# A two-layer transformer block on one core: the second layer's first attention turns its weights three steps behind the scores

## The reference, cut to what matters

```python
def diff_attend(q, k, v, lam):
    s = jnp.einsum('bqhmd,bkhmd->bhmqk', q, k).astype(jnp.float32) * (A_QK ** -0.5)
    p = jax.nn.softmax(s, axis=-1)
    a = p[:, :, 0] - lam * p[:, :, 1]
    return jnp.einsum('bhqk,bkhd->bqhd', a, v.astype(jnp.float32))
...
o = lax.map(lambda qb: diff_attend(qb, k_all, v_all, lam), q_blocks)
out_a = diff_attention_post(o, subln, lam_init).astype(px.dtype) * jax.nn.silu(ga)
out_b = short_conv(bb, cb, ub, conv_w) * jax.nn.silu(gb)
...
oc = diff_attend(qc.reshape(B, L, A_HEADS, 2, A_QK), kc, vc, lam)
```

## Time and profile before

| | |
|---|---|
| Time, median of 3 runs | 1456.33 us (1453.93 to 1456.85) |
| Profiled execution, its time | 1454.62 us |
| Profiled execution, its span | 1452.8 us |
| TensorE busy | 1321.8 us, 91% |
| VectorE, ScalarE, GpSimd busy | 660.0, 625.3, 445.8 us |
| Mean granted clock of TensorE | 0.965 |
| The attention's 48 steps | 767.2 to about 973 us |

### The profile page before, as it was taken

How to read it: one execution, slowest core, us unless ns; L and a number is a source line. 1 busy time by engine, 2 the same in 40 slices (tenths; PEclk the granted TensorE clock), 3 DMA queues, 4 the chain that set the end, 5 groups by cost and what they waited for, 6 DMA issues and landing times.

```text
span 1452.8 us, 19794 instructions
## 1 busy us (share of the span) xinstructions
PE 1321.8 (91%) x7300; PEld 1026.2 (71%) x7300; DVE 660.0 (45%) x1276; ACT 625.3 (43%) x1323; POOL 445.8 (31%) x360
## 2 busy tenths in 40 slices
PE   7999798999999987859998999999998699999995
PEld 6767576676668665648877777778886578677774
DVE  2244784665521505252085676561621721565423
ACT  4434222665442225342226566653433522655432
POOL 2324233322234331322222333332232233222331
PEclk9999899999999998969999999999999799999998
DMA  4212143110143261434123422002121342121441
GB/s 182 84 58 88 59 169 129 64 45 30 59 145 116 105 257 62 171 110 137 59 80 105 109 65 79 30 33 85 59 102 58 131 145 87 59 88 59 175 116 58
DMA packets 27870, 139.89 MB, mean 96 GB/s; under 512 B 4096, under 2 KB 5760, under 8 KB 15232
## 3 DMA queue, kind: packets, MB, share of 16 engines
q1 hardware_dynamic: 20640, 115.43, 22.9%
q10 hardware_dynamic: 7136, 23.19, 4.9%
HBM read 122.87 MB, written 6.29 MB: 89 GB/s over the span
## 4 chain that ended last, share of the span: by engine, by line
PE 70%; DVE 11%; ACT 8%; issue 4%; DMA 3%; POOL 2%; SPq 1%; ACTq 0%; DVEq 0%; POOLq 0%
PE psum L607 48%; PE psum L635 4%; DMA w_raw<-stream 2%; POOL w_low L1079 2%; PE psum L746 2%; ACT q_masked L1250 2%; PE psum L595 2%; ACT w_high L1229 2%; PE psum L830 2%; PE psum L926 1%; PE psum L816 1%; PE psum L1023 1%; PE psum L1037 1%; PE psum L677 1%; PE psum L910 1%
## 5 line engine op out<-in xcount | busy, mean ns | idle before, releaser
L1079 POOL TENSOR_TENSOR w_low<-w_raw,w_high 128x512 fp32r<-128x512 f32 x296 | 390.3, 1329 | 851.4 <-ACT w_high L1229 851.1
L1229 ACT CAST w_high<-w_raw 128x512 fp32r<-128x512 f32 x296 | 178.4, 621 | 485.9 <-PE psum L607 336.1
L607 PE MATMUL psum<-x_high,w_high 128*128 128x512 f32 (+1 forms) x600 | 254.7, 424 | 17.1 <-DVE k_low L1868 8.9
L607 PE MATMUL psum<-x_low,w_high 128*128 128x512 f32 (+1 forms) x600 | 239.4, 399 | 0.0
L607 PE MATMUL psum<-x_high,w_low 128*128 128x512 f32 (+1 forms) x600 | 239.4, 399 | 0.0
L607 PEld LDWEIGHTS psum<-x_high,w_high 128*128 128x128 f32 (+1 forms) x600 | 113.3, 189 | 68.9 <-issue 30.5
L607 PE MATMUL psum<-w_high,x_high 128*128 128x512 f32 (+1 forms) x352 | 141.4, 402 | 13.3 <-ACT w_high L1229 7.6
L607 PE MATMUL psum<-w_low,x_high 128*128 128x512 f32 (+1 forms) x352 | 137.7, 391 | 0.0
L607 PE MATMUL psum<-w_high,x_low 128*128 128x512 f32 (+1 forms) x352 | 137.5, 391 | 0.0
L607 PEld LDWEIGHTS psum<-x_high,w_low 128*128 128x128 f32 (+1 forms) x600 | 113.2, 189 | 28.2
L607 PEld LDWEIGHTS psum<-x_low,w_high 128*128 128x128 f32 (+1 forms) x600 | 113.4, 189 | 21.0 <-issue 1.4
(11 more groups left out here) (312 smaller groups left out, 2459.0 us busy)
## 6 DMA issues: line engine op xcount, KB each, us to landing
w_raw<-stream SPq DMA_DIRECT2D x98, 1024.0 KB, 4.8
x_kept<-arena ACTq DMA_DIRECT2D x8, 512.0 KB, 4.2
arena<-x_kept ACTq DMA_DIRECT2D x8, 512.0 KB, 5.7
arena<-bias ACTq DMA_DIRECT2D x8, 512.0 KB, 3.9
q_masked<-e_q_high SPq DMA_DIRECT2D x24, 96.0 KB, 2.2
arena<-x SPq DMA_DIRECT2D x4, 512.0 KB, 5.2
arena<-x ACTq DMA_DIRECT2D x4, 512.0 KB, 6.9
arena<-ctx ACTq DMA_DIRECT2D x4, 512.0 KB, 4.8
```

Source lines behind the costliest of these rows:

```text
L607: mm = pe.matmul(o, l, r, start=(first and n == 0 and kind != "fc"), stop=(last and n == len(passes) - 1))
L1079: pool.tensor_tensor(WL[:, u % ROOM, :], RAW[:, g % 2, u % 4, :], WH[:, u % ROOM, :].bitcast(F32), ALU.subtract).then_inc(w_lo, 1)
L1229: act.copy(WH[:, u % ROOM, :], RAW[:, g % 2, u % 4, :]).then_inc(w_hi, 1)
```

## The change

The turn of a step, with its copy on ScalarE, goes from two steps behind its score to three. The values of a duo go from even steps to the odd ones that follow. A fourth buffer of the first map, in `TAB`, takes turns with the three of `E_P`; the exponential of the first map then waits for the turn of step s-4. Behind the steps there is one more turn to place among the units of `gc`; the last values stand behind unit 5 instead of unit 3, and the pairs of `ms` behind units 5, 6 and 7 instead of 4, 5 and 6.

```diff
@@ -480,7 +480,8 @@
         six_of = lambda q: [q[:, j, 0:S] for j in range(4)] + [q[:, 2 * n:2 * n + 2, S:] for n in range(2)]
         six_wide = lambda t: [t[:, i, :] for i in range(4)] + [pair(t[:, i, :]) for i in range(4, 6)]
         SIX = (0, 1, 4, 2, 3, 5)
-        map_place = lambda s, m: E_P[:, 3 + s % 2 if m else s % 3, 0:keys_of(s)]
+        FIRST_MAPS = [E_P[:, n, :] for n in range(3)] + [TAB.rearrange("p a n -> p (a n)")]
+        map_place = lambda s, m: (E_P[:, 3 + s % 2, :] if m else FIRST_MAPS[s % 4])[:, 0:keys_of(s)]
 
 
 
@@ -930,31 +931,35 @@
             pieces, n = (piece for chunk in SLIM for piece in slim(chunk)), len(EVEN)
             for s in range(n):
                 score_even(s)
-                if s >= 2:
-                    turn_even(s - 2, 0)
-                if s >= 4 and s % 2 == 0:
-                    values_even((s - 4) // 2)
+                if s >= 3:
+                    turn_even(s - 3, 0)
+                if s >= 5 and s % 2:
+                    values_even((s - 5) // 2)
                 feed("e", pieces, FEED_E[s % 4][0])
-                if s >= 2 and EVEN[s - 2][0]:
-                    turn_even(s - 2, 4)
+                if s >= 3 and EVEN[s - 3][0]:
+                    turn_even(s - 3, 4)
                 feed("e", pieces, FEED_E[s % 4][1])
 
 
             pool[0] = APART_E
+            turn_even(n - 3, 0)
+            unit("gc", 0, X, C)
+            turn_even(n - 3, 4)
+            unit("gc", 1, X, C)
             turn_even(n - 2, 0)
             values_even(n // 2 - 2)
-            unit("gc", 0, X, C)
+            unit("gc", 2, X, C)
             turn_even(n - 2, 4)
-            unit("gc", 1, X, C)
+            unit("gc", 3, X, C)
             turn_even(n - 1, 0)
-            unit("gc", 2, X, C)
+            unit("gc", 4, X, C)
             turn_even(n - 1, 4)
-            unit("gc", 3, X, C)
-            values_even(n // 2 - 1)
-            for k in range(4, NK):
+            for k in range(5, NK):
                 unit("gc", k, X, C)
-                if k < NK - 1:
-                    for i in range(2 * (k - 4), 2 * (k - 4) + 2):
+                if k == 5:
+                    values_even(n // 2 - 1)
+                if k >= 5:
+                    for i in range(2 * (k - 5), 2 * (k - 5) + 2):
                         pe.wait_ge(sig("sq"), i + 1)
                         key = ("ms", SIX[i])
                         acc = open_bank(key, 4 + i % 2)
@@ -1564,8 +1569,8 @@
 
             def exps_even(s, m):
                 key, w, c = ("e", "S", s, m), keys_of(s), 2 * (s % 4) + m
-                if m == 0 and s >= 3:
-                    filled(act, ("e", "T", s - 3, parts_of(s - 3)[-1]))
+                if m == 0 and s >= 4:
+                    filled(act, ("e", "T", s - 4, parts_of(s - 4)[-1]))
                 if m == 1 and s >= 2:
                     act.wait_ge(sig("e_p"), s - 1)
                 act.wait_ge(sig("e_neg"), 2 * s + m + 1)
@@ -1598,27 +1603,30 @@
 
             n = len(EVEN)
             for s in range(n):
-                if s >= 2:
-                    turned_even(s - 2, 0)
+                if s >= 3:
+                    turned_even(s - 3, 0)
                 exps_even(s, 0)
                 exps_even(s, 1)
-                if s >= 2 and EVEN[s - 2][0]:
-                    turned_even(s - 2, 4)
-                if s >= 4 and s % 2 == 0:
-                    values_even((s - 4) // 2)
+                if s >= 3 and EVEN[s - 3][0]:
+                    turned_even(s - 3, 4)
+                if s >= 5 and s % 2:
+                    values_even((s - 5) // 2)
                 if s:
                     fed_even(s - 1)
                     high(fed["e"][2 * s - 1] + ROOM)
             gate_units = UNITS["gc"]
+            turned_even(n - 3, 0)
+            high(fed["e"][2 * n - 1] + ROOM)
+            turned_even(n - 3, 4)
+            high(gate_units[0] + ROOM)
             turned_even(n - 2, 0)
             values_even(n // 2 - 2)
-            high(fed["e"][2 * n - 1] + ROOM)
+            high(gate_units[1] + ROOM)
             turned_even(n - 2, 4)
-            high(gate_units[0] + ROOM)
+            high(gate_units[2] + ROOM)
             turned_even(n - 1, 0)
-            high(gate_units[1] + ROOM)
+            high(gate_units[3] + ROOM)
             turned_even(n - 1, 4)
-            high(gate_units[2] + ROOM)
             values_even(n // 2 - 1)
             act.wait_ge(sig("conv_in_read"), 8)
             act.dma_start(E_BROW, dram["rows"][4:5, :].broadcast_to((P, D))).then_inc(sig("gate_rows0_in"), 16)
```

## The result

The changed kernel takes 1446.62 us (median of 5 runs, 1444.81 to 1448.83) against 1456.33 (5 runs, 1451.64 to 1456.87): ratio 0.9942, interval 0.9923 to 0.9961. A second comparison gave 1446.05 against 1453.69 (23 runs of before): 0.995, interval 0.9931 to 0.9969. So the change takes 7 to 10 us off, 0.5 to 0.6%. One execution of an experiment, the profiled one of the fourth buffer alone, was disturbed as a whole (6,002 us), so its trace is not read.

What follows compares the result with a forecast made beforehand. TensorE, busy for 91% of the span, was taken as the bound, so only its work or waiting counts. 7.0 us gained in attention less 3.2 before `e_ga` gave 3.8: 1456.33 to 1452.5, range 1448.5 to 1457.7.

Steps and rivals of the forecast that it cites:

- The start: Attention before the first pair's step 4: one turn less there, 0.24 us off.
- first stretches: Score of pair step 4 to that of step 10, four times: 25.3 instead of 26.57 us, 5.08 off in all.
- The chain by way of GpSimd's low weights: Pair step 4: low weights (2.54 us) delay the second map's scaling, then VectorE's difference; the turn waits 1.17.
- second stretch: Score of pair step 10 to the next pair's step 4: 0.58 us off 25.15, three times, 1.74 together.
- The 0.6 for turns of six transposes in place of turns of two: Cost counted against the gain between step 10 and the next pair's step 4: 0.6 us at most per moved turn.
- the tail: End of `gc`: ScalarE's sigmoids come late behind the last means, so `e_ga` waits 3.2 us, bounds 1.8 and 4.8.
- the 0.51: Behind the attention's last score: the late wait for a turn's bank, 0.51 us, goes.
- The clock: Rival, chance 0.12: the wait before `e_ga` makes the clock fall to half, 1454.1 us; 1450.9 if only the old fall vanishes.
- No tail wait: Rival, chance 0.17: sigmoids come in time before `e_ga`, all 7.0 us are kept, 1449.3.
- Waits handed on: Rival, chance 0.15: scores after step 6 wait for VectorE's queue instead, step 4 to 10 gains nothing, 1457.7 us.
- slower: Rival, chance 0.09: the attention gains nothing, the 3.2 us wait before `e_ga` stands alone, 1459.5.
- The Trainium skill's drain behind a change of table: ScalarE before the gates' sigmoids: about 1.38 us added, wait before `e_ga` 4.6, forecast 1453.9; the trace didn't bear it out.

## Why the prediction was wrong

**The starting point.** I took 1456.33 us, the median of three runs. The larger sets of runs of before, taken later, have 1453.69, 1454.4 and 1454.61. The span of the profiled execution fits these better. Against those sets the forecast and its range stood some 2 us too high. The first comparison has 1456.33 again, but the same three runs are among its five; its gain is 9.7.

**The start and the first stretches held.** 0.20 for 0.24; 25.23 for the forecast 25.3, a wait of 0.90 to 0.97 at step 7 for 0.5 to 1, none at step 10, VectorE's block passing the gain on. The chain by way of GpSimd's low weights was right in place and size, as the kernels with low weights later show.

**The step that failed is the second stretch:** "0.94 + 0.24 - 0.6 = 0.58 off 25.15". It is 1.26, three times. The 0.6 for turns of six transposes in place of turns of two was mis-sized. In pair steps 1 and 3 before and after differ by the 24 value products alone (3.01 and 4.65 us, 2.59 and 4.24, from one score to the next): they cost 1.65. From the score of pair step 2 to that of 3 before took 5.39 and after 3.01, 2.38 less. Of that 0.94 is the wait and 1.65 the values, so the four more transposes cost 0.21. I had added modelled ends, which overlap (0.66 for four), where the start of one group to that of the next is what TensorE pays. Some 0.27 more went around the scores of steps 0 and 10, which I had not listed. The same kind of term was in the tail: the put-off turn was to be paid with 0.6. The late means cost 3.08 in the kernel that has nothing else changed, and with the 0.51 gone and 2.93 lost in all the turn is left with 0.36.

**What this step explains, and what it does not.** The second stretches are 2.04 of the 2.72 by which the traces beat the sum, the first stretches 0.36, the tail 0.36, the start -0.04. The measured 1446.62 is 5.9 us under the forecast: 2.7 of it are these terms, and 3.2 lie in the starting point and in what the clock did, which no run separates. With every term of the sum right, the forecast would have been 1449.8, still above the first measurement; from 1453.69 it would have been 1447.2, for 1446.05.

**The tail held:** the new wait stands in the forecast place, sigmoid and product come at the forecast distance, and the part costs 2.93 net for 3.29.

**The clock.** Both traces of the changed kernel have a fall behind the wait before `e_ga` (1010.4 and 1008.4 us) and one had it at step 1; before had one behind step 10. Over all experiments six traces have this wait, and four of them a fall behind it. I gave a fall there a chance of 0.12, which was too low, and left out of the range that the old ones would go. Eight waits of a score of 1.4 us or more that stand in traces of kernels with the old step 10 (before and late means) had two falls behind them; the values on even steps had three in four. The waits of 0.9 to 1.0 at step 7 had none in the four traces of the changed attention. How much of the measured gain this is can't be told from so few traces; that the change turns waits of 1.5 us into waits of at most 1.0, and that no fall followed these, is shown.

**The rivals.** No tail wait: false. Waits handed on and slower: false for the change as made; the kernel with values on even steps shows that they were near, with the turns alone moved. The Trainium skill's drain behind a change of table (ScalarE: Activation LUTs, What ACT_TABLE_LOAD costs) again did not show: 1006.85 + 1.28 is 1008.13, the sigmoid starts at 1008.14.

**What I did not see** is that the wait of step 10 had the same root as that of the turn, the low weights in GpSimd's queue: I took VectorE's block from step 7's maxima to step 9's as fixed. With low weights later it is 9.91 us instead of 11.01.

## What to carry to other kernels

When an engine waits for a chain, look at what stands ahead of the chain's link in its own queue before deepening the pipeline: here it was worth 13.5 us to move 2.5 us of work, made up to four units before it is needed, from ahead of a 1 us link to behind it; the deeper pipeline was worth 7 to 10. When steps are moved, follow each engine's queue to the end of the stage, where the last steps meet the banks of the next chunk; and price small matmuls from the start of one group to the start of the next. A median of three runs is a poor anchor for a change of half a per cent.

## What the runs showed of the hardware

VectorE's last operation of the convolution, 255 wide, took 1.39 us in the changed kernel and 1.58 before, against 0.48 for the same operation when the low weights stand elsewhere. The kernel with low weights later, GpSimd and then VectorE:

```profile
835.03 2.55 POOL L1079 TENSOR_TENSOR w_low<-w_raw,w_high 128x512 fp32r<-128x512 f32 x2
...
853.65 3.23 POOL L1079 TENSOR_TENSOR w_low<-w_raw,w_high 128x512 fp32r<-128x512 f32 x2
```

```profile
836.34 2.06 DVE L2247 SCALAR_TENSOR_TENSOR arena<-arena,small 128x768 f32<-128x768 f32 x1
...
842.61 1.82 DVE L2235 TENSOR_REDUCE small<-psum 128x1 f32<-128x768 f32 x2 [0.78 <-PE psum L902]
...
852.04 0.48 DVE L2253 SCALAR_TENSOR_TENSOR e_conv<-e_conv_in,cols_sb,e_conv 128x255 f32<-128x255 f32 x1
...
854.24 1.52 DVE L2247 SCALAR_TENSOR_TENSOR arena<-arena,small 128x768 f32<-128x768 f32 x1
```

Before, the 255-wide operation and GpSimd's pair of subtractions; then the operation in the changed kernel:

```profile
856.36 1.58 DVE L2252 SCALAR_TENSOR_TENSOR e_conv<-e_conv_in,cols_sb,e_conv 128x255 f32<-128x255 f32 x1
...
856.35 2.73 POOL L1079 TENSOR_TENSOR w_low<-w_raw,w_high 128x512 fp32r<-128x512 f32 x2 [2.84 <-ACT w_high L1229]
```

```profile
850.13 1.39 DVE L2260 SCALAR_TENSOR_TENSOR e_conv<-e_conv_in,cols_sb,e_conv 128x255 f32<-128x255 f32 x1
```

Where a VectorE operation with two SBUF inputs meets a GpSimd subtraction of low weights, one or both of them take longer in these rows. Before, the operation ran from 856.36 to 857.94; the first subtraction of the GpSimd pair ends at about 857.66, and 0.28 later the operation ends. With low weights later the differences that meet subtractions take 2.06 and 1.52 for 1.01, and of the two pairs one takes 3.23 and the other its usual 2.55. The Trainium skill (GPSIMD Engine Reference, Specifications) says that GpSimd's SBUF interfaces are shared with VectorE and that VectorE's instructions with two SBUF inputs contend for them; the trace agrees, and prices one such meeting at 0.5 to 1.1 us for VectorE.

In the kernel before, the meeting stood in the middle of the block that set step 10's wait. The rows tell its share: from step 7's maxima to step 9's VectorE takes 11.01 before and 9.91 with low weights later (842.61 to 852.52), 1.10 less, and the 255-wide operation is 1.10 shorter. A first stretch is 2.02 shorter, 26.57 to 24.55; the other 0.92 is that step 7's maxima start 12.37 behind the score of step 4 instead of 13.29. That is why the gain passed the forecast for that run. A kernel that moves only the second of these low weights was not run, so the split rests on the rows.
